# First attention of a three-block kernel: stacked q and k tiles written per head by ScalarE and VectorE, with fixed bias rows picked by a selector

## What is computed

```python
def _fox_attention(x, w_in, b_f, w_out):
    proj = x @ w_in                                # q, k, v, and one gate column per head
    f_logit = proj[..., 3 * d:] + b_f
    c = jnp.cumsum(jax.nn.log_sigmoid(f_logit), axis=1).transpose(0, 2, 1)
    def block(i):
        logits = jnp.einsum('bhqd,bhkd->bhqk', qb, k) * scale
        logits = logits + cb[..., :, None] - c[..., None, :]
        mask = kpos[None, :] <= qpos[:, None]
        p = jax.nn.softmax(jnp.where(mask, logits, -jnp.inf), axis=-1)
        return jnp.einsum('bhqk,bhkd->bhqd', p, v)
    o = lax.map(block, jnp.arange(s // Q_BLOCK))
    return _merge_blocks(o) @ w_out
```

## Time and profile before

| | us |
|---|---|
| median of 3 runs | 2031.44 |
| lowest and highest of them | 2029.02, 2041.62 |
| profiled execution, time | 2035.9 |
| profiled execution, span of its trace | 2034.1 |

### The profile page before, as it was taken

The page is one execution under the profiler, slowest core; times in us unless marked ns, Lnnn a source line. Parts: engine busy times, 40 slices in busy tenths (PEclk is TensorE's granted clock), DMA queues, the critical chain, the costliest instruction groups (busy, mean ns, idle before and its releaser), DMA issues.

```text
span 2034.1 us, 25951 instructions
## 1 busy us (share of the span) xinstructions
PE 1866.7 (92%) x8169; PEld 1496.3 (74%) x8169; DVE 861.2 (42%) x1340; ACT 806.0 (40%) x1605; POOL 1036.9 (51%) x879
## 2 busy tenths in 40 slices
PE   6777899999988999989999999798988889999997
PEld 5556688888856888767888888566666668888885
DVE  6997300001233555583333232455555653333234
ACT  4322332232233455434444422555555254444223
POOL 5784656555552232255666655534342456666552
PEclk8898899999988999989999999799998889999998
DMA  4211233332323444222333233221211223332331
GB/s 136 62 42 43 73 102 93 95 92 86 92 81 83 117 112 124 73 83 76 100 93 97 84 93 94 57 56 42 52 46 52 63 63 94 102 93 86 90 93 62
DMA packets 325350, 166.51 MB, mean 82 GB/s; under 512 B 42338, under 2 KB 317876, under 8 KB 325300
## 3 DMA queue, kind: packets, MB, share of 16 engines
q1 hardware_dynamic: 323954, 165.29, 28.8%
q10 hardware_dynamic: 1346, 0.59, 0.1%
HBM read 151.10 MB, written 2.10 MB: 75 GB/s over the span
## 4 chain that ended last, share of the span: by engine, by line
PE 67%; issue 14%; DVE 10%; POOL 4%; ACT 4%; DMA 0%; POOLq 0%; SPq 0%; ACTq 0%; DVEq 0%
PE bank L709 21%; PE bank L711 21%; PE bank L710 21%; POOL WL L564 3%; DVE work L1459 2%; DVE vconv L1459 2%; POOL XL L594 1%; ACT work L1317 1%; PE score L789 1%; DVE pmap L1670 1%; DVE small L1556 1%; PE score L801 1%; ACT xres L1091 1%; ACT XH L1090 1%; PE score L901 1%
## 5 line engine op out<-in xcount | busy, mean ns | idle before, releaser
L564 POOL TENSOR_TENSOR WL<-raw,WH 128x512 fp32r<-128x512 f32 (+2 forms) x656 | 804.8, 1249 | 821.5 <-ACT WH L1065 821.5
L709 PE MATMUL bank<-XL,WH 128*128 128x512 f32 x1600 | 651.3, 407 | 53.7 <-POOL XL L594 16.3
L711 PE MATMUL bank<-XH,WL 128*128 128x512 f32 x1600 | 636.4, 398 | 0.0
L710 PE MATMUL bank<-XH,WH 128*128 128x512 f32 x1600 | 635.8, 397 | 0.0
L1065 ACT ACTIVATE WH<-raw 128x512 fp32r<-128x512 f32 (+2 forms) x656 | 342.5, 571 | 610.2 <-PE bank L711 606.9
L709 PEld LDWEIGHTS bank<-XL,WH 128*128 128x128 f32 x1600 | 309.1, 193 | 121.0 <-POOL XL L594 18.2
L711 PEld LDWEIGHTS bank<-XH,WL 128*128 128x128 f32 x1600 | 307.7, 192 | 66.4
L710 PEld LDWEIGHTS bank<-XH,WH 128*128 128x128 f32 x1600 | 309.3, 193 | 59.2
L711 PE MATMUL bank<-HH,WL 128*128 128x512 f32 x528 | 208.8, 395 | 0.0
L710 PE MATMUL bank<-HH,WH 128*128 128x512 f32 x528 | 208.8, 395 | 0.0
L709 PE MATMUL bank<-HL,WH 128*128 128x512 f32 x528 | 208.7, 395 | 0.0
(11 more groups left out here) (215 smaller groups left out, 2170.5 us busy)
## 6 DMA issues: line engine op xcount, KB each, us to landing
raw<-in_ffn_w_in SPq DMA_DIRECT2D x88, 512.0 KB, 3.8
raw<-in_ffn_w_out SPq DMA_DIRECT2D x32, 384.0 KB, 3.2
raw<-in_w_gate SPq DMA_DIRECT2D x22, 512.0 KB, 3.8
raw<-in_w_up SPq DMA_DIRECT2D x22, 512.0 KB, 3.8
raw<-in_ffn_w_out SPq DMA_DIRECT2D x32, 320.0 KB, 3.1
raw<-in_a_w_in SPq DMA_DIRECT2D x16, 512.0 KB, 4.0
raw<-in_kv_w SPq DMA_DIRECT2D x32, 256.0 KB, 2.9
raw<-in_w_in SPq DMA_DIRECT2D x12, 512.0 KB, 4.5
```

Source lines behind the costliest of these rows:

```text
L564: pool.tensor_tensor(WL[:, s, ks, :], raw[:, g.slot(RAW), ks, :], WH[:, s, ks, :].bitcast(F32), ALU.subtract).then_inc(w_lo, 1)
L709: pe.matmul(out_, wh, xl, start=start, stop=False)
L710: pe.matmul(out_, wh, xh, start=False, stop=False)
L711: return pe.matmul(out_, wl, xh, start=False, stop=stop)
```

## The change

ScalarE writes the high parts of q straight into QX and those of k into KB, per head, as two operations on 64 partitions; VectorE writes the low parts into QX and KX, two operations as well. Two DMAs per unit copy the high parts to their second place, QX to QB and KB to KX. The single-row copies of the bias go: VectorE writes the high and low bias rows of all 16 heads into KB's partitions 64 to 127 once, ahead of the stage, with zeros between. Which head's rows count is picked in QB: GpSimd copies two columns of a table `hot` over QB, once ahead of the stage and once per unit for the next one, and the score matmul takes all 128 rows. PE's wait for `bias_ones` ahead of the first product becomes one for `cc_ready` at 4, the bias rows of KB. ScalarE loads one function table for Exp and Ln ahead of the gate.

```diff
@@ -235,6 +235,7 @@
         wf = sb("wf", [P, DT, FOX_HEADS], stack=fox)
+        hot = sb("hot", [P, FOX_HEADS + 2], stack=fox)
         QX = sb("QX", [P, 2, 2, S], F32R, stack=fox)
@@ -253,8 +254,6 @@
         CC = work[:, 5, :].bitcast(F32R)
-        part_h = [work[:, 1 + j, :].bitcast(F32R) for j in range(2)]
-        part_l = [work[:, 3 + j, :].bitcast(F32R) for j in range(2)]
         back = ExitStack()
@@ -316,7 +315,8 @@
         gate_a, gate_b = sem("gate_a"), sem("gate_b")
-        bias_ones = sem("bias_ones")
+        hot_ready = sem("hot_ready")
+        bias_in = sem("bias_in")
         q_packed, k_packed = sem("q_packed"), sem("k_packed")
@@ -490,32 +490,14 @@
             def pack_q(u):
-                turn = STAGES["qkv1"][1] + 4 * u
-                sp.wait_ge(bank_read[0], turn // 2 + 1)
-                for e in range(2):
-                    r = slice(HEAD * e, HEAD * e + HEAD)
-                    sp.dma_start(QX[0:HEAD, u % 2, e, :].bitcast(F32), part_h[0][r, :].bitcast(F32)).then_inc(q_packed, 16)
-                    sp.dma_start(QX[HEAD:P, u % 2, e, :].bitcast(F32), part_l[0][r, :].bitcast(F32)).then_inc(q_packed, 16)
-                    sp.dma_start(QB[0:HEAD, u % 2, e, :].bitcast(F32), part_h[0][r, :].bitcast(F32)).then_inc(q_packed, 16)
+                sp.wait_ge(bias_in, u + 1)
+                sp.wait_ge(qk_hi, 4 * u + 2)
+                sp.dma_start(QB[0:HEAD, u % 2, :, :].bitcast(F32), QX[0:HEAD, u % 2, :, :].bitcast(F32)).then_inc(q_packed, 16)
             def pack_k(u):
-                turn = STAGES["qkv1"][1] + 4 * u + 1
-                if u:
-                    for c in range(2):
-                        sp.wait_ge(s_done[c], 4 * u)
-                else:
-                    sp.wait_ge(cc_ready, 2)
-                for e in range(2):
-                    for lo in range(2):
-                        h = 32 * lo + 2 * u + e
-                        sp.dma_start(KB[HEAD + lo:HEAD + lo + 1, e, :].bitcast(F32), CC[h:h + 1, :].bitcast(F32)).then_inc(k_packed, 16)
-                sp.wait_ge(bank_read[1], turn // 2 + 1)
-                for e in range(2):
-                    r = slice(HEAD * e, HEAD * e + HEAD)
-                    sp.dma_start(KX[0:HEAD, e, :].bitcast(F32), part_l[1][r, :].bitcast(F32)).then_inc(k_packed, 16)
-                    sp.dma_start(KX[HEAD:P, e, :].bitcast(F32), part_h[1][r, :].bitcast(F32)).then_inc(k_packed, 16)
-                    sp.dma_start(KB[0:HEAD, e, :].bitcast(F32), part_h[1][r, :].bitcast(F32)).then_inc(k_packed, 16)
+                sp.wait_ge(qk_hi, 4 * u + 4)
+                sp.dma_start(KX[HEAD:P, :, :].bitcast(F32), KB[0:HEAD, :, :].bitcast(F32)).then_inc(k_packed, 16)
             def fox_load(u, j):
@@ -664,11 +646,19 @@
             lows_of_x(2, lambda t: xres[:, t, :])
-            pool.memset(QB[:, :, :, :].bitcast(F32), 1.0).then_inc(bias_ones, 1)
-
-            with pool.Fori(0, UNITS) as it:
-                for j in range(4):
-                    low(Nth(STAGES["qkv1"][0] + j + 2, it, 4), (UNIT[2:] + UNIT[:2])[j])
+            def bias_rows(slot, heads):
+
+                pool.tensor_copy(QB[:, slot, :, :], hot[:, heads].unsqueeze(2).broadcast_to([P, 2, S])).then_inc(bias_in, 1)
+
+            pool.wait_ge(hot_ready, 1)
+            bias_rows(0, slice(0, 2))
+            with pool.Fori(0, UNITS // 2) as it:
+                for c in range(2):
+                    u = Nth(c, it, 2)
+                    for j in range(4):
+                        low(u.times(4, STAGES["qkv1"][0] + j + 2), (UNIT[2:] + UNIT[:2])[j])
+                        if j == 2:
+                            bias_rows(1 - c, bass.ds(it * 4 + 2 * c + 2, 2))
             lows("out1", 2, 4)
@@ -689,7 +679,7 @@
                     if j < 2 and iu is not None:
-                        pool.wait_ge(qk_hi, iu.times(2, 2 * UNITS + j).n(1))
+                        pool.wait_ge(qk_hi, iu.times(2, 4 * UNITS + j).n(1))
                         pool.tensor_tensor(QKL[:, iu.slot(2), j, :], qk[:, :], QKH[:, iu.slot(2), j, :].bitcast(F32),
                                            ALU.subtract).then_inc(qk_lo, 1)
@@ -909,7 +899,7 @@
                 pe.matmul(sc[c][:, k], QX[:, slot, e, q], KX[:, e, k], start=True, stop=False)
-                pe.matmul(sc[c][:, k], QB[0:HEAD + 2, slot, e, q], KB[0:HEAD + 2, e, k], start=False, stop=False)
+                pe.matmul(sc[c][:, k], QB[:, slot, e, q], KB[:, e, k], start=False, stop=False)
                 pe.matmul(sc[c][:, q], identr[:, :], masks[:, 0, :], start=False, stop=True).then_inc(s_done[c], 1)
             def turn_map(b, used, src, i):
@@ -955,8 +945,11 @@
                         if sl == 0:
-                            pe.wait_ge(q_packed, u.times(16 * 6).n(16 * 6))
-                            pe.wait_ge(k_packed, u.times(16 * 10).n(16 * 10))
+                            pe.wait_ge(bias_in, u.n(1))
+                            pe.wait_ge(q_packed, u.times(16).n(16))
+                            pe.wait_ge(k_packed, u.times(16).n(16))
+                            pe.wait_ge(bank_read[0], u.times(4, STAGES["qkv1"][1]).round(2, 1))
+                            pe.wait_ge(bank_read[1], u.times(4, STAGES["qkv1"][1] + 1).round(2, 1))
                         score_packed(sl, u.times(4, sl // 2), slot, sl // 2)
@@ -983,7 +976,7 @@
                     weave(unit_steps("qkv1", iu), fox_slot(au), FOX_STEPS)
             pe.wait_ge(consts, CONSTS)
-            pe.wait_ge(bias_ones, 1)
+            pe.wait_ge(cc_ready, 4)
             weave_units(pe.Fori, fox_part)
@@ -1173,6 +1166,8 @@
             norm_rms(2, lambda t: xres[:, t, :])
+            act.add_instruction(mybir.InstLoadActFuncSet(name=nc.get_next_instruction_name(), act_func_set_id=LN_EXP_SET,
+                                                         engine=mybir.EngineType.Activation, ins=[], outs=[]))
             act.wait_ge(gate_a, 1)
@@ -1223,15 +1218,14 @@
                             act.wait_ge(item_done, iu.times(4, STAGES["qkv1"][0] + j + 1).n())
-                            if au is not None:
-                                act.wait_ge((q_packed, k_packed)[j], iu.times(16 * (6, 10)[j]).n())
-                            act.activation(part_h[j], bank[j][:, :], ACT.Copy,
-                                           scale=1.0 if j else HEAD ** -0.5).then_inc(qk_hi, 1)
+                            for e in range(2):
+                                act.activation(KB[0:HEAD, e, :] if j else QX[0:HEAD, iu.slot(2), e, :],
+                                               bank[j][HEAD * e:HEAD * e + HEAD, :], ACT.Copy,
+                                               scale=1.0 if j else HEAD ** -0.5).then_inc(qk_hi, 1)
                         if j == 3:
                         unit_high("qkv1", iu, j)
-            act.wait_ge(cc_ready, 2)
             weave_units(act.Fori, fox_part)
@@ -1536,6 +1530,8 @@
             norm(2, "g_final", False, True)
+            dve.tensor_tensor(hot[:, :], ident[:, HEAD:HEAD + FOX_HEADS + 2], ident[:, HEAD + 32:HEAD + 32 + FOX_HEADS + 2],
+                              ALU.add).then_inc(hot_ready, 1)
             dve.wait_ge(gate_done, 1)
@@ -1546,9 +1542,13 @@
             own.link(dve.tensor_tensor_scan(z, osq[0:FOX_HEADS, :], e, 0.0, ALU.mult, ALU.add))
-            dve.tensor_copy(CC[0:FOX_HEADS, :], z).then_inc(cc_ready, 1)
-            dve.wait_ge(cc_ready, 1)
-            dve.tensor_tensor(CC[32:32 + FOX_HEADS, :], z, CC[0:FOX_HEADS, :].bitcast(F32), ALU.subtract).then_inc(cc_ready, 1)
+            own.did(dve.tensor_copy(CC[0:FOX_HEADS, :], z))
+            own.link(dve.memset(KB[HEAD:P, :, :].bitcast(F32), 0.0))
+            for e in range(2):
+                dve.tensor_copy(KB[HEAD:HEAD + FOX_HEADS, e, :], z).then_inc(cc_ready, 1)
+                dve.tensor_tensor(KB[HEAD + 32:HEAD + 32 + FOX_HEADS, e, :], z, CC[0:FOX_HEADS, :].bitcast(F32),
+                                  ALU.subtract).then_inc(cc_ready, 1)
+            dve.wait_ge(cc_ready, 4)
             def row_max(n, used):
@@ -1590,12 +1590,15 @@
                         j = sl // 4 - 1
-                        dve.wait_ge(qk_hi, iu.times(2, j).n(1))
-                        dve.scalar_tensor_tensor(out=part_l[j], in0=bank[j][:, :], scalar=1.0 if j else HEAD ** -0.5,
-                                                 in1=part_h[j].bitcast(F32), op0=ALU.mult,
-                                                 op1=ALU.subtract).then_inc(bank_read[j], 1)
-
-            dve.wait_ge(cc_ready, 2)
+                        for e in range(2):
+                            dve.wait_ge(qk_hi, iu.times(4, 2 * j + e).n(1))
+                            h = KB[0:HEAD, e, :] if j else QX[0:HEAD, iu.slot(2), e, :]
+                            ins = dve.scalar_tensor_tensor(
+                                out=KX[0:HEAD, e, :] if j else QX[HEAD:P, iu.slot(2), e, :], in0=bank[j][HEAD * e:HEAD * e + HEAD, :],
```

(4 more changed lines are left out.)

## The result

| | before | after |
|---|---|---|
| median of 20 runs each, us | 2032.13 | 2039.92 |
| lowest and highest, us | 2026.83, 2042.32 | 2034.53, 2042.47 |
| profiled execution: time, span, us | 2035.9, 2034.1 | 2042.4, 2040.6 |

The ratio is 1.0034, with a 95% interval of 1.0022 to 1.0045: slower by 0.34%, about 7 us, where 1.3 us was forecast. The forecast time was 2032.7 us, the measured one is 2039.92: inside the range of 2026 to 2040.5, near its upper end. "Within 1%" came true; the size of the loss did not.

The account below looks back on a forecast made before the run. The prediction took PE, nearly always busy in the first attention's loop, as the bound. Stage head -2.6 plus loop +3.9 gave +1.3 us, hence 2032.7 us from a median of 2031.44; range 2026 to 2040.5.

Parts of the forecast that it names:

- step 3: Head of the stage: two stretches at PE's low clock become one behind the gap at the start, -2.5 us.
- Step 5: Loop, slots 4 and 8: VectorE's second half delays PE in slot 4, 0.55 for each of seven units, +3.9 us.
- rival (b): Loop: ScalarE's and VectorE's delays add up, 1.2 in each of seven units, total +5.8, 2037.2 us; chance 0.12.
- Step 1: Stage start: PE waits for VectorE's bias rows before the first q product, starting at 617.6 against 610.97, +6.6 us.
- Step 2: Unit 0's first score: PE's idle time there goes if the two copies land in time, -7.7 us.
- B + 8.1: Unit 0: when PE needs the k copy, in us after B, ScalarE's first read of the q product.
- Rival (c): Unit 0: the 256 KB copy behind a weight load lands 2 us too late, total +3.3, 2034.7 us; chance 0.11.
- Step 4: Unit 0's small costs: +0.5 us waiting for v's weights, +0.5 for the copy of v.
- rival (d): VectorE loses the overlap of neighbouring operations when rows change, 1.7 in the loop, total +3.3, 2034.7 us; chance 0.10.
- Step 6: GpSimd's selector copy is hidden in its idle time, the 128-row score matmul costs the same, fewer SP issues gain nothing.

Follow-up runs that it names:

- experiment 2: Changed kernel with VectorE's low part of q's second head moved from slot 4 to slot 6; 2035.51 us, ratio 1.0011 to the kernel before.
- experiment 3: Changed kernel with PE's bias-row wait at the first score and q's second low half in slot 6; 2020.88 us, ratio 0.9949 to the kernel before.
- experiment 7: Kernel before, with PE's wait for QB's ones at the first score and SP waiting for them before its first copy into QB; 2024.9 us, ratio 0.9974.
- Experiment 6: Kernel before, with PE also waiting for VectorE's bias rows in CC ahead of the stage's first product; ratio 1.0037.
- experiment 1: Changed kernel with PE's wait for KB's bias rows moved from the first product to unit 0's first score; 2024.48 us, ratio 0.9955 to the kernel before.
- experiment 9: As experiment 8, with SP in unit 0 alone issuing the copy of k ahead of a weight load; ratio 0.9952 to the kernel before.
- experiment 10: Changed kernel with GpSimd copying the selector's columns once more per unit into an unread spare tile; 2039.61 us, ratio 1.0032 to the kernel before.
- experiment 8: As experiment 3, but with both low halves of q out of slot 4, in slots 6 and 7; 2023.32 us, ratio 0.9961 to the kernel before.
- experiment 4: Kernel before, with VectorE making the low part of q in slot 4 once more, on all rows, into an unread spare tile; ratio 1.0029.
- experiment 5: Kernel before, with VectorE making the low part of q in slot 4 as two operations, rows 0 to 63 and 64 to 127; ratio 1.0049.

## Why the prediction was right and where it was not

**The number and the range.** The direction and "within 1%" were right; two of the terms were not (steps 3 and 5). That the time lies inside the range is in part luck: the terms, taken at their worst, ended at 2038.7, and only the 1.5 to 2 us that were added for the scatter of the runs reach 2039.92. The nearest of the numbers named was rival (b)'s 2037.2, whose mechanism experiment 2 refutes.

**What bounds the kernel, and that this can't show as faster.** Right: the most to be won at the copies was put at 11 us, and what they bring (experiments 3 and 7) is 5 by the timed runs and 7 to 8 by the traces.

**Step 1, the early wait: +6.6, measured +6.8.** Right in mechanism and size. The memset took 0.91 for 0.96, and no table load stands between Exp and Ln (610.22 + 0.63, Ln at 610.88). VectorE's tensor_scalar took 1.25 us beside GpSimd's copy, in experiment 3 it took 0.41 when the copy was over before it; but Ln was done only at 611.51, so the hold was covered. Experiment 6 shows that such a wait alone costs 7.5 us with what follows it (4.7 in the trace).

**Step 2, the idle time at the first score: -7.7, measured -7.7.** Right in the number, by luck in its last 0.8 us. The copy of k lands 5.4 us after its issue in unit 0, behind a weight load, where 3.2 to 4.3 was said. It fitted only since PE itself came later, at B + 9.6 (631.26 to 640.87) for the B + 8.1 of the forecast, and what made it later is the second stretch at the low clock of step 3. In experiment 1, which has no such stretch, PE waits 0.8 for this copy, and experiment 9 takes that wait away. Rival (c) is thus right in its mechanism, and the clock hid it in this kernel.

**Step 3, the clock: -2.5, measured about -0.5 (worked out below).** This step failed. It counted one stretch behind one gap. There were two: behind the wait for v's weights, 1.82 us, stood another 3.4 us at 0.50. The traces of experiments 2 and 10, which keep the early wait, show the same: 1.8 us of waiting for v's weights, then 3.4 us at 0.50. Experiments 1, 3, 8 and 9 have the same wait of 1.8 us and no such stretch; there PE had not stood still before it. Experiment 6 has the early wait (8.21 us) with a shorter one for v's weights (1.27), and no stretch behind the second. So neither the 1.8 us without the early wait nor the early wait with 1.27 brings it in these traces; what decides was not tried. The stretches of before cost 1.6 and 3.3; those of after 2.7 and 1.7, all taken as half their length. (Products start 0.43 us apart at the low clock and 0.23 at the high one, 1.9 times and not twice; the difference of the two sums stays the same.) The step looked at the gaps that the change makes and removes, and not at the one between, which it lengthens by half a microsecond.

**Step 4, small costs.** The wait for v's weights grew from 1.27 to 1.82 (+0.55, said 0.5). The copy of v is waited for in seven units (+0.4, said 0.5). The clock that followed the first of them is under step 3.

**Step 5, the loop: +3.9, measured +5.7** (0.82 in seven units; the first, 28.11, has it as well). The place of the work was right, and that PE had no slack for it: the work of slot 8 is covered, as said, and that of slot 4 is not. Where it arrives was seen only in part: 0.61 at slot 6, and 0.21 at slot 8, which the forecast did not look at. The size was off: 0.55 for a half, where experiment 4 measures 0.62 for an operation and experiment 5 0.22 more for the rows. That is rival (d), to which 0.10 was given, and it should have been a part of the sum: the next start 0.08 ahead of an end, lost at three places, gives 0.24 (it is lost at two, 0.09 and 0.13). The Trainium skill, "VectorE: DVE Perf Modes", section "Two Vector instructions with no wait between them", has an instruction held until the earlier ones have finished when it begins in another group of 32 partitions than the one that last used the same memory. Experiments 4 and 5 agree with it in the trace, 1.21 for two operations on the same rows against 1.42. The give-back that the forecast took off, from GpSimd's hold, is real in slot 6 (the normalising took 0.53 for 0.74, in experiment 4 0.42) and worth nothing in the end: VectorE and ScalarE carry the whole delay on to slot 8, and PE waits for it there.

**Step 6, hidden.** Right (experiment 10). The copy takes 1.04 us, near the lower bound of 0.9, and the score matmul with 128 rows for 66 has a median of 310 ns where it was 336.

The sum with the measured terms: 6.8 - 7.7 - 0.5 + 0.55 + 0.4 + 5.7 = +5.3, and +1.4 stands in rows of the account that the change doesn't touch, against +6.5 between the two spans. That is 0.2 more than measured, which stays unexplained. Of the forecast's error of some 5 us (+1.3 forecast, +6.5 between the traces) the loop's price made 1.8 and the clock 2.0; the rest is the 1.4 in those two rows, within their scatter.

## What to carry to other kernels

A wait that must come before some work should stand at that work, not at the start of the stage: here it cost 10 us of idleness and, with the low clock, some 4 us more, and moving one line turned a slower kernel into a faster one (1.0034 to 0.9955). Before adding an operation to a half-idle engine, look at the slot where it goes: if what it does next is already waited for, all of it counts, and it belongs where the engine waits for somebody else. Follow a delay to the last place where another engine meets it: what is given back at the first one (0.2 to 0.3 us here) can be asked for again at the next. Splitting an operation by rows doubled its price here, and added a little more for the move to other rows and back.

## What the hardware showed that was not expected

- Two VectorE operations on 128x512 stand 0.61 us apart; on rows 0 to 63 and then 64 to 127 they stand 0.70 apart, and the next one on all rows 0.73 behind the second (experiments 4 and 5). Nothing is won by half the rows.
- In the changed kernel a gap of 1.82 us in PE's work was followed by 3.4 us at the low clock. In experiment 3 the gap for v's weights is of 1.8 us too, and the clock stayed at 1.00 from 606 to 832 us. So the gap alone does not decide. Three traces have the stretch (with those of experiments 2 and 10), four have the same gap and not the stretch.
- A DMA of 256 KB from one part of the on-chip memory to another landed in 2.9 us, one with half the bytes in 2.3; behind a weight load, in unit 0, it took 5.4.
- A VectorE operation on 128x18 took 1.25 us while GpSimd was at work beside it, and one on 16x512 took 1.25 beside GpSimd's copy where it took 0.41 without (experiment 3).
